# A hybrid decoder layer on eight cores: four tiles side by side at the start, the spatial weights loaded first

## The reference

```
mod = silu(c) @ w_ada + b_ada                  # shift, scale, gate, twice: 6 x 1024
h   = rms(x) * g_mix * (1 + sc1) + sh1
u, v, B, C, hin = h @ w_in                     # 5 x 512 columns
v   = rms_per_head(gelu(v)) * g_v              # 8 heads of 64
a   = gelu(u) * (tril(w_s[head]) @ v + b_s)    # within chunks of 128 tokens
b   = B * conv3(C * hin)                       # causal, depthwise, width 3
x1  = x + gt1 * (concat(a, b) @ w_out)
h2  = rms(x1) * g_ffn * (1 + sc2) + sh2
y   = rms(x1 + gt2 * (relu(h2 @ w_ff1)^2 @ w_ff2)) * g_final
```

## Time and profile before

| | |
|---|---|
| time, median of 3 runs | 809.09 us (808.39 to 809.74) |
| the profiled execution's own time | 815.89 us |
| its span on the slowest core (core 1) | 814.4 us |
| spans of the eight cores | 794.4 to 814.4 us |
| TensorE busy | 728.6 us (89%) |
| VectorE, ScalarE, GpSimd busy | 368.9 us, 271.0 us, 142.1 us |
| phase A ends, about | 330 us |

### The profile page before, as it was taken

How to read it: one execution, slowest core, us unless ns; L and a number is a source line. 1 busy time by engine, 2 the same in 40 slices (tenths; PEclk the granted TensorE clock), 3 DMA queues, 4 the chain that set the end, 5 groups by cost and what they waited for, 6 DMA issues and landing times.

```text
span 814.4 us, 16945 instructions; the slowest of 8 cores (794.4 to 814.4 us)
## 1 busy us (share of the span) xinstructions
PE 728.6 (89%) x6232; PEld 506.5 (62%) x6232; DVE 368.9 (45%) x762; ACT 271.0 (33%) x530; POOL 142.1 (17%) x154
## 2 busy tenths in 40 slices
PE   1453999997999999799999999999999999999996
PEld 0342687755576767674794684774774864855854
DVE  0232567754657666331453453443433533533523
ACT  2152435512233422240342351451441441532511
POOL 5302302434355442200010000000000000000000
PEclk9997999999999999989999999999999999999999
DMA  8999997999898859996020110200200200200001
GB/s 144 155 205 178 192 157 110 179 204 246 168 245 152 227 86 210 177 191 102 28 79 2 52 57 1 103 3 27 78 2 27 78 1 27 79 2 27 27 1 52
DMA packets 46983, 83.05 MB, mean 102 GB/s; under 512 B 2204, under 2 KB 31654, under 8 KB 46902
## 3 DMA queue, kind: packets, MB, share of 16 engines
q0 software_dynamic: 32304, 36.70, 32.8%
q1 hardware_dynamic: 14598, 45.27, 17.7%
HBM read 101.73 MB, written 16.96 MB: 146 GB/s over the span
## 4 chain that ended last, share of the span: by engine, by line
PE 76%; DMA 13%; issue 3%; DVE 3%; ACT 2%; POOL 1%; SPq 0%; DVEq 0%; POOLq 0%; ACTq 0%
PE ps L316 68%; DMA arena<-w_in 5%; PE ps L870 3%; DMA arena<-x_p 3%; DMA arena<-w_s 3%; DVE arena L327 2%; ACT arena L321 2%; PE ps L436 1%; DMA mod_scr<-arena 1%; DVE arena L324 1%; POOL arena L324 1%; PE ps L714 1%; PE ps L737 1%; PE ps L560 1%; POOL arena L99 0%
## 5 line engine op out<-in xcount | busy, mean ns | idle before, releaser
L316 PE MATMUL ps<-arena 128*128 128x256 bf16 (+1 forms) x4408 | 637.9, 306 | 22.0 <-DVE arena L324 13.5
L316 PEld LDWEIGHTS ps<-arena 128*128 128x128 bf16 x4408 | 430.3, 99 | 216.3 <-issue 35.1
L324 POOL TENSOR_TENSOR arena<-arena 128x1 f32<-128x1 f32 (+3 forms) x100 | 107.4, 1077 | 612.3 <-DVE arena L397 476.5
L324 DVE TENSOR_TENSOR arena<-arena 128x256 bf16<-128x256 f32 (+5 forms) x353 | 158.9, 460 | 116.1 <-ACT arena L321 106.8
L321 ACT ACTIVATE arena<-ps,arena 128x256 f32<-128x256 f32 (+1 forms) x320 | 147.0, 472 | 147.8 <-PE ps L316 97.2
L321 ACT ACTIVATE arena<-arena 128x256 f32<-128x256 f32 (+4 forms) x101 | 76.9, 772 | 232.8 <-DVE arena L324 154.3
L324 DVE TENSOR_TENSOR arena<-ps,arena 128x512 f32<-128x512 f32 (+6 forms) x98 | 59.5, 610 | 193.4 <-PE ps L316 147.2
L327 DVE SCALAR_TENSOR_TENSOR arena<-arena 128x256 f32<-128x256 f32 (+4 forms) x118 | 96.1, 822 | 30.7 <-POOL arena L324 23.0
L321 ACT ACTIVATE arena<-ps 128x1024 bf16<-128x1024 bf16 (+5 forms) x56 | 45.7, 819 | 153.1 <-PE ps L436 92.4
L327 DVE SCALAR_TENSOR_TENSOR arena<-ps,arena 128x256 bf16<-128x256 f32 (+1 forms) x64 | 30.9, 483 | 25.1 <-PE ps L316 13.1
L436 PE MATMUL ps<-arena 128*128 128x128 bf16 x256 | 19.8, 230 | 15.6 <-DVE arena L327 15.5
(11 more groups left out here) (88 smaller groups left out, 119.0 us busy)
## 6 DMA issues: line engine op xcount, KB each, us to landing
arena<-x_p SPq DMA_DIRECT2D x32, 512.0 KB, 10.2
arena<-w_ff POOLq DMA_DIRECT2D x16, 1024.0 KB, 26.3
arena<-w_ada POOLq DMA_DIRECT2D x12, 1024.0 KB, 33.0
x_scr<-arena SPq DMA_DIRECT2D x16, 512.0 KB, 9.3
arena<-x_scr SPq DMA_DIRECT2D x16, 512.0 KB, 4.5
y_p<-arena SPq DMA_DIRECT2D x14, 512.0 KB, 2.7
arena<-w_in POOLq DMA_DIRECT2D x5, 1024.0 KB, 64.3
arena<-w_out POOLq DMA_DIRECT2D x2, 1024.0 KB, 92.1
```

The lines of the kernel that those rows point to most:

```text
L316: ins = e.matmul(out, lhsT=l, rhs=r, start=(i == 0), stop=(i == n - 1))
L324: S.op(eng, lambda e: e.tensor_tensor(out=out, in0=in0, in1=in1, op=op), reads=reads, writes=writes)
```

## The change

Four tiles run side by side at the start, so that tile 3's u, v and spatial steps stand between those of the others, and `conv(t3)` follows `conv(t2)`; the call `steady(3, ...)` is gone and `reload` and `wout` of tile 0 stand in its place. Tile 3 gets an `hT` buffer of its own in the place of the buffer X4, and the X buffers of the second loads are swapped. `x` of tile 0 and `w_s` are among the first transfers of SP, and the mask, `setup_spatial` and `setup_spatial_pe` stand ahead of the bias of u. One gelu of one column comes behind the two silus. The list `pending` is packed into fewer entries. The whole diff:

```diff
--- before.py
+++ after.py
@@ -188,7 +188,9 @@
     assert cur[0] <= f1w[7][2]
     cur[0] = f1w[4][2]
     X45 = [take("X%d" % i, D, F32) for i in (4, 5)]
-    slot4_b = [t[1] for t in X45]
+
+    hT3 = (view(X45[0][2], 8 * TILE, BF16), Buf("hT3"), X45[0][2])
+    slot4_b = [t[1] for t in X45] + [hT3[1]]
     hT2 = take("hT2", 8 * TILE, BF16)
     Csb2 = [take("Csb%d" % i, TILE, F32) for i in (2, 3)]
     accb2 = [take("acc%d" % i, TILE, F32) for i in (2, 3)]
@@ -247,7 +249,7 @@
     bF, _, _ = take("bF", 32, F32)
     bF_b = bufs("bF0", "bF1")
     hbs = [take("hb%d" % i, D, BF16) for i in range(2)]
-    hT = [take("hT%d" % i, 8 * TILE, BF16) for i in range(2)] + [hT2]
+    hT = [take("hT%d" % i, 8 * TILE, BF16) for i in range(2)] + [hT2, hT3]
     g1B, g1B_b, _ = take("g1B", D, F32)
     gt1B, gt1B_b, _ = take("gt1B", D, F32)
     identb, identb_b, _ = take("identb", 128, BF16)
@@ -878,9 +880,9 @@
 
 
     NT = SEQ // TILE
-    tA = [dict(kind="A", i=i, row0=i * TILE, x=(2 if i in (1, 3) else 0), h=(0, 1, 2, 0, 1, 0, 1, 0)[i], xr=(4, 2, 4, 2, 4, 2, 2, 2)[i],
+    tA = [dict(kind="A", i=i, row0=i * TILE, x=(2 if i in (1, 3) else 0), h=(0, 1, 2, 3, 0, 1, 0, 1)[i], xr=(2, 4, 2, 4, 2, 4, 2, 2)[i],
                x1b=bufs("x1s_%d_0" % i, "x1s_%d_1" % i)) for i in range(NT)]
-    tB = [dict(kind="B", i=i, row0=i * TILE, x=(2 * i) % 4, h=(i + 1) % 2, x1b=tA[i]["x1b"]) for i in range(NT)]
+    tB = [dict(kind="B", i=i, row0=i * TILE, x=(2 * i) % 4, h=i % 2, x1b=tA[i]["x1b"]) for i in range(NT)]
 
 
     cS, cS_b = vgs[0][0][:, 0:128], vgs[0][1]
@@ -907,6 +909,8 @@
         S.dma("pool", w_in_g[nm], win_src[:, :, lo:lo + 512], [], [win_b[nm]], win_b[nm].name)
 
 
+    for j in range(2):
+        n_load(tA[0], j)
     load(cS, c_s.rearrange("t (k n) -> (t k) n", k=8), [cS_b], "cS")
     load(cP, c_p.rearrange("o (k n) -> (o k) n", k=8), [cP_b], "cP")
     for i, (lo, n, src) in enumerate((
@@ -914,8 +918,7 @@
             (56, 8, g_ffn.rearrange("o (r n) -> (o r) n", n=128)), (64, 8, g_final.rearrange("o (r n) -> (o r) n", n=128)),
             (72, 4, g_v.rearrange("o (r n) -> (o r) n", n=128)), (76, 12, w_conv.rearrange("j (c n) -> (j c) n", n=128)))):
         load(st88[lo:lo + n, :], src, [st88_b[i]], st88_b[i].name)
-    for j in range(2):
-        n_load(tA[0], j)
+    load(wst3, w_s.rearrange("h t s -> t h s"), wst_b, "wst")
     ada_dma(2)
     ident(identf, identf_b)
     ada_dma(3)
@@ -937,6 +940,7 @@
 
     act(cS, cS, AF.Silu, [cS_b], [cS_b])
     act(cP, cP, AF.Silu, [cP_b], [cP_b])
+    act(xout[:, 0:1], mhalf[:, 0:1], AF.Gelu_apprx_tanh, [mhalf_b], [xout_b])
     bk, bkb = next_bank()
 
     def tr_c(e, bk=bk):
@@ -980,7 +984,6 @@
     for j in range(2):
         n_load(tA[2], j, after=[win_b["u"]])
     load(gvB, g_v.partition_broadcast(128), [gvB_b], "gvB")
-    load(wst3, w_s.rearrange("h t s -> t h s"), wst_b, "wst")
 
     def setup_spatial():
         S.op("pool", lambda e: e.memset(ind2[0:2, :], 1.0), reads=[ind2_b], writes=[ind2_b])
@@ -1025,7 +1028,10 @@
 
 
     t0, t1, t2, t3 = tA[0:4]
+    S.op("pool", lambda e: e.affine_select(out=wst3, in_=wst3, compare_op=ALU.is_ge, fill=0.0, base=0,
+                                           pattern=[[0, 8], [-1, 128]], channel_multiplier=1), reads=wst_b, writes=wst_b)
     setup_spatial()
+    setup_spatial_pe()
     win_bias("u")
     for j in range(2):
         n_stats(t1, j)
@@ -1033,10 +1039,10 @@
         A_u(t0, c)
     for j in range(2):
         n_mod(t1, j)
+    for j in range(2):
+        n_load(t3, j)
     load(xS, x_s.rearrange("t (k n) -> (t k) n", k=8), [xS_b], "xS", after=[win_b["C"]])
     load(scS, sconv.rearrange("t (j n) -> (t j) n", j=8), [scS_b], "scS")
-    S.op("pool", lambda e: e.affine_select(out=wst3, in_=wst3, compare_op=ALU.is_ge, fill=0.0, base=0,
-                                           pattern=[[0, 8], [-1, 128]], channel_multiplier=1), reads=wst_b, writes=wst_b)
     for j in range(2):
         n_tr(t1, j)
     v_bias()
@@ -1049,34 +1055,43 @@
     for j in range(2):
         n_mod(t2, j)
     for j in range(2):
+        A_vn(t0, j)
+        A_v(t1, j)
+    for j in range(2):
         n_tr(t2, j)
-    for j in range(2):
-        n_load(t3, j)
-        n_load(tA[4], j)
-    setup_spatial_pe()
-    for j in range(2):
-        A_vn(t0, j)
-    for j in range(2):
-        A_v(t1, j)
+        n_stats(t3, j)
     for j in range(2):
         A_spatial(t0, j)
     for c in range(4):
         A_u(t2, c)
     for j in range(2):
+        n_mod(t3, j)
         A_vn(t1, j)
     for j in range(2):
         A_v(t2, j)
     for j in range(2):
+        n_load(tA[4], j)
         A_spatial(t1, j)
     for j in range(2):
+        n_tr(t3, j)
+    for c in range(4):
+        A_u(t3, c)
+    for j in range(2):
         A_vn(t2, j)
+    for j in range(2):
+        A_v(t3, j)
+    for j in range(2):
+        A_spatial(t2, j)
     win_bias("C")
     win_bias("h")
-    for c in range(4):
+    A_ch(t0, 0)
+    for j in range(2):
+        A_vn(t3, j)
+    for c in range(1, 4):
         A_ch(t0, c)
     win_bias("B")
     for j in range(2):
-        A_spatial(t2, j)
+        A_spatial(t3, j)
     for c in range(4):
         A_b(t0, c)
     setup_sample()
@@ -1099,10 +1114,13 @@
         do(at_3)
         A_b(tl, 3)
 
-    conv(t1, None, [lambda: n_stats(t3, 0)], [lambda: n_stats(t3, 1)], None)
-    conv(t2, [lambda: n_mod(t3, 0), lambda: n_mod(t3, 1), lambda: ada_cols(4), lambda: ada_dma(8)],
-         [lambda: n_tr(t3, 0), lambda: n_stats(tA[4], 0)], [lambda: n_tr(t3, 1), lambda: n_stats(tA[4], 1)],
-         [lambda: ada_cols(5), lambda: ada_dma(9)])
+    t4, t5 = tA[4:6]
+    conv(t1, None, [lambda: n_stats(t4, 0)], [lambda: n_stats(t4, 1)], None)
+    conv(t2, [lambda: n_mod(t4, 0), lambda: n_mod(t4, 1), lambda: n_load(t5, 0), lambda: n_load(t5, 1), lambda: ada_cols(4), lambda: ada_dma(8)],
+         [lambda: n_tr(t4, 0)], [lambda: n_tr(t4, 1)], [lambda: ada_cols(5), lambda: ada_dma(9)])
+    conv(t3, [lambda: ada_row(2), lambda: bcast_load(2, gt1B, gt1B_b), lambda: s_sq(xsT, xsT_b)], [lambda: n_stats(t5, 0)],
+         [lambda: s_rs()], [lambda: n_stats(t5, 1)])
+    alias_after([X45[0][1]], [hT3[1]])
     ff1_dma(7)
     ff1_dma(5)
 
@@ -1172,35 +1190,30 @@
     DA_ = lambda q: (lambda: ada_dma(q))
     pending.extend([
 
-        lambda: (ada_row(2), bcast_load(2, gt1B, gt1B_b), s_sq(xsT, xsT_b)),
-        ada_job(6, DA_(10)),
-        lambda: s_rs(),
+        lambda: (ada_job(6, DA_(10))(), s_mod(xsT, xsT_b, 1, 0)),
         ada_job(7, DA_(11)),
-        lambda: s_mod(xsT, xsT_b, 1, 0),
-
+        lambda: [s_win(g) for g in range(2)],
         ada_job(8, D1(0)),
-        lambda: [s_win(g) for g in range(2)],
+        lambda: ([s_win(g) for g in range(2, 5)], s_elem1(), s_v1()),
+
         ada_job(9, D1(1)),
-        lambda: ([s_win(g) for g in range(2, 5)], s_elem1(), s_v1()),
-        lambda: ada_row(4),
-
-        lambda: s_v2(),
+        lambda: (ada_row(4), s_v2()),
         lambda: (ada_job(10, D1(2))(), s_v3()),
         lambda: s_zout(ncs[:, 512:1024].rearrange("t (c n) -> t c n", c=4)),
         lambda: (ada_job(11, D1(3))(), s_v4()),
-        lambda: ada_row(5),
 
         lambda: s_wout(),
-        lambda: (s_zout(nvs.rearrange("t (c n) -> t c n", c=4)), s_sq(x1sT, x1sT_b)),
+        lambda: (ada_row(5), s_zout(nvs.rearrange("t (c n) -> t c n", c=4)), s_sq(x1sT, x1sT_b)),
         lambda: s_rs(),
-        lambda: ff1_dma(4),
+        None,
         lambda: s_mod(x1sT, x1sT_b, 4, 3),
 
-        lambda: s_ff1(0),
+        lambda: (ff1_dma(4), s_ff1(0)),
         lambda: (s_ff1(1), alias_after([f1Ts_b], [xsT_b, zhist_b]), s_relu(0)),
         lambda: ff1_dma(6),
     ])
-    steady(3, None, tA[0], tA[4], tA[5])
+    reload(tA[0])
+    wout(tA[0])
     steady(4, tA[1], tA[2], tA[5], tA[6])
     steady(5, tA[3], tA[4], tA[6], tA[7])
     steady(6, tA[5], None, tA[7], tB[0])
```

## The result

The changed kernel takes 819.67 us (median of 4 runs, 818.77 to 823.13), the one before 808.74 beside it (807.87 to 809.74). The ratio is 1.013, with a 95% interval of 1.0104 to 1.0157: it is slower by 1.3%, 10.9 us. The forecast was 803.4, the range 797 to 812. The profiled execution took 819.55 us with a span of 818.0 on core 2. The kernels of the experiments ran on three chips, each beside the kernel before, and their times stand as ratios to it; it took 808.3, 813.0 and 808.1 us there. In some executions of every kernel one die or both ran at a lower granted clock and the time was longer; ratios and means leave these out.

A forecast was written before the change was run, and what follows sets the result against it. TensorE's early idle time was taken as the bound, chiefly core 1's 12.70 us wait from queue order. 16.4 us removed, less 4 (a), 3.7 (b) and 3 (c), gave 5.7 off the median 809.1: 803.4, range 797 to 812.

The forecast's parts named there:

- The wait is a queue's order and goes: Before tile 2's transposes on TensorE: waits for weights it doesn't use, behind GpSimd's mask; 13.0 us removed.
- The slowest core is core 1, with its 12.70 us: Basis of the sum: core 1, span 814.4, sets the time and still ends last after the change; 5.7 us saved.
- (a): First transfers: spatial weights ahead of ada, u and v make u and v land net 4 us later (52 and 61).
- (b): ScalarE's order at tiles 2 and 3: copy, square, copy leave TensorE idle 2.2 and 1.5 us, sum 3.7.
- (c): Join to the steady part: w_out of tile 0 directly follows conv of tile 3; net cost 3 us, from -3.4 to +9.
- Rival C: Join: broadcast and x of tile 0 take 16 us each in series, TensorE idles 12 us net; 812, chance 0.18.
- D: Stops inside matmul runs, as in the sample tokens' projection (3.59 us), can go or double; 3 to 6 us, range only.
- the sentence on the packed list: Sample tokens' jobs in 18 slots instead of 23: DMAs move closer, idle stretch at 134 to 142 covers; otherwise 6.5 us.

The follow-up runs named there:

- The new front order: Tile 2's modulation ahead of v of tile 0, its transposes ahead of v of tile 1, on the changed kernel with block 4 back: ratio 0.9919 to the kernel before.
- block 4 back: Changed kernel with the load of ff1 block 4 returned to its earlier slot, in tile 6's iteration: ratio 1.0019 to the kernel before.
- both repairs: Changed four-tile kernel with ff1 block 4 at its old place and tile 2's modulation and transposes moved earlier: ratio 0.9919 to the kernel before.
- the weights alone: Kernel before, three tiles, with x and w_s among the first transfers and mask and setup ahead of u's bias: ratio 0.999.
- after: The changed kernel itself, four tiles and block 4 late, against the kernel before: 819.67 us, ratio 1.013.

## Why the prediction was wrong

It said faster by 5.7 us; the kernel is slower by 10.9. Point by point:

- *The wait is a queue's order and goes.* Right: 12.70 to 0.42 us, and moving the mask alone takes it down too. But I credited all 13.0 us of it. With the weights there, 3.97 us remain in three tiles, by VectorE's order alone; the sum for four tiles charged for that only what ScalarE did.
- *The slowest core is core 1, with its 12.70 us.* Wrong as a basis. It was so in one profiled execution, and I took its saving off the median of all. In 59 other executions of the kernel before, core 1 was the slowest in 5. The mean wait of the eight cores was 9.5 us, 3.5 less than was credited; by that the same sum gives 2.2 us and not 5.7. (Core 4's gain in the sum is 5.7 less the 4.24 us between the two waits, 1.5 us and not 1.2.)
- *(a) u and v 4 us later.* Right: 52.4 and 62.8 against 52 and 61; over all profiles 4.0 and 4.3 us later. The 1.2 us that were estimated from the Trainium skill (DMA: Bandwidth & Descriptors, Specifications) are not what the runs show.
- *(b) the order on ScalarE, 3.7 us.* Mis-sized. Copy, square, copy and the wait before u of tile 2 (3.01 for 2.2) and of tile 3 (1.94 for 1.5) are near the forecast. What I left out is 4.04 us before the spatial part of tile 0: v of tile 0 is scaled behind tile 2's modulation, and tile 0's spatial part now follows without v of tile 1 in between to cover it. The four waits and the 0.42 are 9.4 us, and the clock, counted at 1.00, was 0.75 from 80 to 90 us and 0.87 from 90 to 110: at 18.07 us of TensorE's work at 0.87 and 2.82 at 0.75 that is 3 us more. From v to the C bias were 49.9 us, where 38.8 were forecast (41.5 less 16.4, 10 for tile 3, 3.7); 5.7 of the 11.1 between them are waits, 3 the clock, and 2.4 I can't assign. The C bias came at 113.40, not at about 100. The new front order is worth 0.8% or 6.6 us with block 4 back.
- *(c) the join, 3 us.* Wrong in sign: the store and the first add came 4.6 and 12.8 us after the row, not 8.9 and 24.5. The store met engines as full as before (1.10 against 1.05), the load of x half busy ones (0.55 against 1.07). From 112 to 250 us TensorE's waits for other engines or transfers fell from 3.7 to 2.3 us on average, a gain of 1.4. Rival C, which was this term grown large, did not happen.
- *D, the stops.* The one in the sample tokens' projection went, 2.6 us on average over the cores before.
- **The step that failed** is the sentence on the packed list: "Their DMAs move closer; cover is the idle stretch of the DMA engines at 134 to 142 (0.27)." I counted bytes at the front and didn't follow the one load whose slot changed. `ff1_dma(4)` went from ahead of `s_mod` to beside `s_ff1(0)`, some 15 us later, past the stretch at 285 to 295 us in which the DMA engines now idle and in which it could have run, into the issue of two ff2 blocks. Block 6 queues behind the three, and TensorE waits for it. The loss is 9.0 us of time and waits of 8.07 to 11.21 us on three cores; the price named there, 6.5 us for a block, is of that order, but it was kept out of the sum, and no rival had it.

This step accounts for 9.0 of the 10.9 us (1.0130 to 1.0019), and for the direction; it does not account for the missing gain. That is the mis-sized (b), the clock and the basis in one core: 16.4 less 3.5 for the mean wait, 4.2 for (a), 9.4 for (b), 3 for the clock, and 1.4 and 2.6 back from the join and the stops, is 0.3 us, ahead of the 2.4 that I can't assign. Measured with block 4 back: the time of the kernel before, within 0.5%. The kernel with both repairs takes an estimated 804 us (819.7 less 9.0 and 6.6), next to the forecast of 803.4, but it is another order of the front than the one forecast, and the agreement is luck.

Three things stay open. Which core gets the long trip of block 6 goes by the pair, as the table shows, but not why; two of the later cores (32.5 and 32.8 us) also lie between the levels, and both issue it 5 to 6 us after their neighbour, as one with 41.8 does too. The crowd of SP's transfers is a part at most; its first half (stores and gate) was not moved. And the 3.9 us that phase A gains with the weights alone come from two profiles, where the same start differs by up to 2.6 us at the C bias; the mean core gained 1.6 us, and whether the slowest one gained nothing or a little, the interval of 0.9956 to 1.0023 leaves open.

## What to carry to other kernels

When a change repacks a list of jobs, compare the issue time of every load in it, before and after, with the first use of the last load behind it in the same queue; here a load that moved past an idle stretch of the DMA engines cost 9.0 us, more than the 6.5 estimated for its bytes. A wait that "goes" leaves the next one in line: find out what the waiting instruction's other inputs have to wait for before crediting its whole length. Add up the waits of a stretch over all cores, before and after: 9.5 and 9.4 us said here at once that the front had gained nothing. Don't take the wait of one core off the time of all when another core is the slowest in the next execution. Where one line undoes a loss, test it in both directions, on both kernels.

## What the runs showed of the hardware

- A 1 MB block with float32 to bf16 on the software queue landed 43.93 us after its issue, behind three others, with the engines moving 169 and 222 GB/s in the two stretches from 340 to 350; issued alone, with other traffic about, block 4 took 10.5 to 13.5 us (6.5 was the estimate from the 161 GB/s of the earlier trace rows).
- With three blocks issued together, the core of each pair (0 and 1, 2 and 3, 4 and 5, 6 and 7) that issues later had the longer trip in 16 of 16 pairs of four kernels: 32.5 to 43.9 us for block 6 against 26.8 to 33.3. That the neighbour's transfers make it so is inferred from this pattern.
- Stops inside runs of matmuls ("issue") of up to 6.6 us fall between 187 and 203, 286 and 295, and 320 and 355 us, on some cores and not on others. The first of these places, in the sample tokens' projection, has them in all six kernels with three tiles (on seven cores of the kernel before) and in none of the six with four. The Trainium skill (Runtime: NRT & Kernel Launch, Instruction fetch mechanics) says that an engine's next block of instructions comes by a DMA queue of its own, mostly hidden. The page of after has that queue (51 packets), and in twelve of the stops, from six kernels, the DMA engines were 0.85 or more busy; that the one makes the other no run here shows.
- Two kernels that end phase A 3.9 us apart had the same time on the slowest core; 9.2 us apart, the time moved by 1.0%, 8.4 us.
